# Forgetting attention: the causal mask is added to the diagonal scores by VectorE in PSUM, in place of TensorE's unit matrix times mask

## The chip, the cores and the metric

The kernel runs on one core of a Trainium2 chip. The metric is the time of one execution on the device in microseconds (us), as the median of several runs. Profiles show one execution.

## The reference, cut to what matters

The program is a chain of three layers over 512 positions of width 1024: a Hyena layer, a layer with gated spatial mixing and forgetting attention, and a layer with pooling and a short convolution. All but the first have cross attention to a memory of 256 positions, and each ends in a gated feed-forward block. The change touches the forgetting attention of the second layer, 8 heads of 64:

```python
def forgetting_attention(q, k, v, log_f):
    c = jnp.cumsum(log_f.astype(jnp.float32), axis=1).transpose(0, 2, 1)
    ...
        logits = jnp.einsum('bqhd,bkhd->bhqk', qi, k).astype(jnp.float32) * scale
        logits = logits + ci[..., :, None] - c[:, :, None, :]
        allowed = kpos[None, :] <= qpos[:, None]
        logits = jnp.where(allowed[None, None], logits, -jnp.inf)
        p = jax.nn.softmax(logits, axis=-1)
        return jnp.einsum('bhqk,bkhd->bqhd', p.astype(v.dtype), v)
```

It is swept in 4 query blocks of 128 (qt = 0 to 3). Block qt sees the keys 0 to 128(qt+1) - 1, and only its last 128 keys, the diagonal block, need the mask.

## The kernel before, in words

Weights stream through the whole program: SyncE loads a block of 1 MB into w_raw, ScalarE copies it in two halves to w_hi (L1866), GpSimd computes the rest w_lo (L2331), and TensorE forms each product from three matmuls (hi hi, hi lo, lo hi; L532 to L534). There are two buffers of each. PSUM is two tensors of four banks, `acc` and `aux`, each used round robin. Each engine has its own instruction list, executed in order; semaphores tie them together.

The forgetting attention takes the heads in 4 pairs. The order of the steps is written out by hand in two lists, FOX_PE for TensorE and ScalarE, and FOX_DVE for VectorE. A step is (what, pair p, query block qt). In the text they are S(p,q), T(p,q), O(p) and R(p,q):

- S(p,q), scores. TensorE opens two acc banks, one for each head, and adds up 6 matmuls of half height (64 rows; L906), 2 that subtract the running sum of log f (40 rows; L910), and 2 of full height that add the mask as unit matrix times mask (L913). With n columns, n = 256, 256, 384, 512 for q = 0 to 3. Because the bank must have at least 256 columns, `mask_0` serves q = 0 and `mask_r` the others. VectorE then takes the negative maximum of each row over both banks (L1613), and ScalarE forms the exponentials into prob_e with that as bias and the row sum on the side (L2188); this frees the banks for the S step after the next.
- R(p,q): VectorE takes the reciprocal of the sums (L1617), and GpSimd scales prob_e with it (L2426). In VectorE's list R stands behind the S step that follows its own.
- T(p,q): TensorE transposes the scaled blocks into aux banks (L609), once they are scaled; VectorE copies them to pt (L1620).
- O(p): TensorE multiplies the turned probabilities of pair p with the values (24 matmuls, L885), ScalarE copies the result to ye_hi (L2195), VectorE computes ye_lo (L1173) and frees the aux bank.
- M: the first matmuls of the projection behind the attention, put in ahead of O(2) to fill a wait.

TensorE's order is S(0,0) to S(0,3), then T(0,0) S(1,0) T(0,1) S(1,1) and so on; for p > 0, O(p-1) stands between T(p,1) and S(p+1,1). VectorE's, for one pair in the middle, is T(p,0) S(p+1,0) T(p,1) R(p+1,0) S(p+1,1) O(p-1) T(p,2) R(p+1,1) S(p+1,2) T(p,3) R(p+1,2) S(p+1,3), and R(p,3) is behind S(p+1,0).

The mask tiles are made once, at about 684 us, by four ScalarE copies (L2112, L2114), from a constant that holds 0 where the key is allowed and -1e30 elsewhere. `step` on VectorE lets its instruction raise a semaphore and waits for it before the next instruction; `for_act` raises the one that ScalarE waits for.

Of the kernel before, what the change touches and what calls it, by code (L numbers as in the profile page):

```python
# [28 lines left out]
P = 128  # L29
# [161 lines left out]
def build(nc, ins, out):  # L191
    F32, F32R, I32 = mybir.dt.float32, mybir.dt.float32r, mybir.dt.int32
    ALU = mybir.AluOpType
    ACT = mybir.ActivationFunctionType
# [7 lines left out]
    def at(name, shape, dtype=F32, offset=None):  # L202

        size = 4 * int(np.prod(shape[1:]))
        if offset is None:
            offset = base[0]
            base[0] = -(-(offset + size) // 32) * 32
        assert offset + size <= END, name
        return nc.alloc_sbuf_tensor_at(name, list(shape), dtype, offset=offset)
# [26 lines left out]
    sq_at = base[0]  # L236
# [6 lines left out]
    def c(name, n, lo=0):  # L243
        return ca[:, CA[name] + lo:CA[name] + lo + n]
# [4 lines left out]
    ident = c("ident", P)  # L249

    def area(start=None):

        pos = [region if start is None else start]

        def put(name, shape, dtype=F32):
            t = at(name, shape, dtype, offset=pos[0])
            pos[0] += -(-4 * int(np.prod(shape[1:])) // 32) * 32
            return t
        return put, pos


    put, _ = area()
# [4 lines left out]
    put, pos = area()  # L267
# [45 lines left out]
    put, _ = area()  # L313
# [3 lines left out]
    put, pos = area()  # L317
# [9 lines left out]
    late, _ = area(v_at)  # L327
    q_raw = late("q_raw", [P, TT, T])
    sel_r = put("sel_r", [104, HEADS], F32R)
    ident_r = put("ident_r", [P, P], F32R)  # L330
    sel_raw = put("sel_raw", [104, HEADS])
    row_small = put("row_small", [P, P])
    masks = at("masks", [P, 3 * P], F32R, offset=sq_at)
    mask_r, mask_0 = masks[:, 0:2 * P], masks[:, P:3 * P]
    assert pos[0] <= region + MIXED_AT
    put, pos = area(region + MIXED_AT)
    late, _ = area(pos[0] + 8192)
# [25 lines left out]
    put, pos = area()  # L363
# [21 lines left out]
    put, _ = area()  # L385
# [5 lines left out]
    put, _ = area(region + MIXED_AT)  # L391
# [5 lines left out]
    acc = ctx.enter_context(nc.psum_tensor("acc", [P, 4, 512], F32))  # L397
# [3 lines left out]
    def sem(name):  # L401
        return ctx.enter_context(nc.semaphore(name))
# [6 lines left out]
    acc_ready = sem("acc_ready")  # L409
# [73 lines left out]
    def _(pe):  # L483
# [413 lines left out]
        for what, p, qt in FOX_PE:  # L897
            n = P * (qt + 1)
            if what == "S":
                banks = [open_acc(("S", p, qt, j)) for j in range(2)]  # L900
                scores[0] += 2
                n = max(n, 2 * P)
                for l, r in ((q_hi, k_hi), (q_hi, k_lo), (q_lo, k_hi)):
                    for j in range(2):
                        rows = slice(HD * j, HD * (j + 1))
                        nc.tensor.matmul(banks[j][:, 0:n], l[rows, p, qt * P:(qt + 1) * P], r[rows, p, 0:n],  # L906
                                         start=l is q_hi and r is k_hi, stop=False)
                for j in range(2):
                    h, rows = 2 * p + j, slice(HD * j, HD * j + 40)
                    nc.tensor.matmul(banks[j][:, 0:n], sel_r[rows, h:h + 1].to_broadcast([40, P]), decay_r[rows, 0:n],  # L910
                                     start=False, stop=False)
                for j in range(2):
                    nc.tensor.matmul(banks[j][:, n - 2 * P:n], ident_r[:, :], mask_r if qt else mask_0,  # L913
                                     start=False, stop=True)                        .then_inc(acc_ready, 1)
            elif what == "T":
                pe.wait_ge(probs_scaled, scaled.next(2))
                tiles = [[prob_e[j][qt][:, kt * P:(kt + 1) * P] for kt in range(qt + 1)] for j in range(2)]
                if qt < 2:
                    transposes(("T", p, qt, 0), tiles[0] + tiles[1])
                else:  # L920
                    for j in range(2):
                        transposes(("T", p, qt, j), tiles[j])
            elif what == "O":
                mixed_values(p)
            else:
                mixed_w = block_in(KT, 256)
                mixed_banks = [open_acc(("mixed", o)) for o in range(2)]
                mixed_out(0, range(4))
# [151 lines left out]
    def _(dve):  # L1080
        V = nc.vector
# [14 lines left out]
        def signal_with(ins, counter):  # L1096
            ins.then_inc(counter.sem, 1)
            counter.next()
            newest[0] = counter
# [6 lines left out]
        def for_act(ins):  # L1106
            signal_with(ins, to_act)
# [186 lines left out]
        for b in range(12):  # L1294
            j, part = b // 3, b % 3
# [210 lines left out]
        for t in range(2):  # L1506
            g_rows = g_tok[:, t, :].rearrange("p (g c) -> p g c", g=4)
            scale = row_small[:, 16 + 4 * t:20 + 4 * t].rearrange("p (g one) -> p g one", one=1).to_broadcast([P, 4, P])
# [94 lines left out]
            return aux[:, (n_aux[0] - 1) % 4, :]  # L1603

        exp_done = {}
        for what, p, qt in FOX_DVE + [("O", PAIRS - 1, 0)]:
            n = P * (qt + 1)
            if what == "S":
                dve.wait_ge(acc_ready, acc_done.next(2))
                b = n_acc[0] % 4  # L1610
                n_acc[0] += 2
                exp_done[p, qt] = acc_read.next(2)
                for_act(V.tensor_reduce(small[:, 8 + 2 * qt:10 + 2 * qt], acc[:, b:b + 2, 0:n], axis=AX.X, op=ALU.max,  # L1613
                                        negate=True))
            elif what == "R":
                dve.wait_ge(acc_free, exp_done[p, qt])
                signal_with(V.reciprocal(small[:, 24 + 2 * qt:26 + 2 * qt], small[:, 16 + 2 * qt:18 + 2 * qt]), inverted)  # L1617
            elif what == "T":
                for j in range(1 if qt < 2 else 2):
                    free_aux(V.tensor_copy(turned(p, qt, j), from_bank(next_aux(), qt)))  # L1620
            else:
                bank = next_aux()
                acted()
                halve(ye_hi[:, 4 + p, :], ye_lo[:, 4 + p, :], bank, last=free_aux)
# [220 lines left out]
    def _(act):  # L1845
        S = nc.scalar
# [25 lines left out]
        def step(ins):  # L1872
            ins.then_inc(act_step, 1)
            act.wait_ge(act_step, steps.next())
# [38 lines left out]
        for k in range(KT):  # L1913
            if k == 2:
                split_next()
            n = mark[("x", k)]
# [36 lines left out]
        for b in range(12):  # L1953
            j, part = b // 3, b % 3
# [94 lines left out]
        for k in range(KT):  # L2049
            n = mark[("x again", k)]  # L2050
# [56 lines left out]
        for i in range(4):  # L2107
# [1 line left out]
                split_next()  # L2109
            evacuated()  # L2110
            S.activation(u_t[:, i, :], tmp[i][:, :], ACT.Gelu_apprx_tanh)
        S.activation(ident_r[:, :], ident, ACT.Copy)  # L2112
        for i, scale in ((0, 0.0), (1, 1.0), (2, 0.0)):
            S.activation(masks[:, i * P:(i + 1) * P], c("mask", P) if scale else ident, ACT.Copy, scale=scale)  # L2114
        act.wait_ge(in_even, 16 * 4)
        S.activation(sel_r[:, :], sel_raw[:, :], ACT.Copy)
        split_next()
        for t in range(TT):
            if t == TT - 1:
                split_next()  # L2120
            n = acc_mark[("g", t)]
# [56 lines left out]
        for what, p, qt in FOX_PE + [("O", PAIRS - 1, 0)]:  # L2178
            n = P * (qt + 1)
            if (what, p) == ("O", PAIRS - 1):  # L2180
                split_next()
            if what == "S":
                given()
                for j in range(2):
                    evac.next()
                    i = 2 * qt + j
# [115 lines left out]
        for j in range(2):  # L2302
# [3 lines left out]
            if j == 0:  # L2306
                for g in range(4):
                    n = mark[("pool", g)]
# [242 lines left out]
```

## Time and profile before

| | |
|---|---|
| median of 3 runs | 1920.89 us (1919.56 to 1921.23) |
| span of the profiled execution, first to last instruction | 1918.7 us |
| median less that span | 2.2 us |
| TensorE, VectorE, ScalarE, GpSimd busy | 1889.0, 956.3, 688.7, 913.3 us |
| granted TensorE clock, mean | 0.999 of full speed |
| the mask matmuls, L913 | 32, between 781.9 and 816.1 us |

The time of the profiled execution outside its span is not in the profile; 2.2 us is the median's distance to it. A matmul's row lasts from its start until its result has arrived; the next one starts earlier, so the time it takes from TensorE's queue is read from start to start. "x2" means that a row merges two instructions.

### The profile page before, as it was taken

Reading aid. Unit: us, or ns where it says so; the run is one execution under the profiler, and the core shown is the slowest. Engines: PE = TensorE matmul, PEld = TensorE weight load, DVE = VectorE, ACT = ScalarE, POOL = GpSimd, SP = SyncE. Lnnn points to the kernel's source line nnn. Section 1 sums busy time; section 2 is a strip of 40 time slices with the busy share of each in tenths; the row PEclk is TensorE's granted clock in tenths of the full one; section 3 lists DMA queues with packets and bytes.
Section 4 is the critical chain, followed back from the end, with each engine's and each line's share of the span. In section 5 each row is a group of like instructions: output and inputs, shape, how many; then the busy total and the mean of one; then the engine's idle time right before and its main releaser. Section 6 shows DMA issues by size and latency. Waiting matters only on the chain.

```text
span 1918.7 us, 22821 instructions
## 1 busy us (share of the span) xinstructions
PE 1889.0 (98%) x8677; PEld 1547.8 (81%) x8677; DVE 956.3 (50%) x1245; ACT 688.7 (36%) x1016; POOL 913.3 (48%) x409
## 2 busy tenths in 40 slices
PE   7999999999999999999999999999999999999999
PEld 6777888888888878778778888888888878888887
DVE  7877945444421248654564444213855484444201
ACT  4556333232323344443633232222234543222211
POOL 2564645444444444644544444445445444445442
PEclk9999999999999999999999999999999999999999
DMA  5241122323323322123232232333243223232322
GB/s 178 67 126 66 67 66 88 109 87 93 101 81 102 117 67 98 36 70 128 67 110 87 94 103 85 102 99 100 82 132 110 87 70 107 88 109 87 99 88 77
DMA packets 165176, 178.91 MB, mean 93 GB/s; under 512 B 4697, under 2 KB 152657, under 8 KB 164850
## 3 DMA queue, kind: packets, MB, share of 16 engines
q1 hardware_dynamic: 162092, 172.10, 27.9%
q10 hardware_dynamic: 3013, 5.84, 1.0%
q8 instruction: 48, 0.79, 0.2%
q14 instruction: 23, 0.18, 0.0%
HBM read 175.83 MB, written 2.10 MB: 93 GB/s over the span
## 4 chain that ended last, share of the span: by engine, by line
PE 60%; issue 21%; POOL 12%; DVE 4%; ACT 2%; DMA 0%; POOLq 0%; DVEq 0%; ACTq 0%
PE acc L532 18%; PE acc L534 18%; PE acc L533 18%; POOL w_lo L2331 11%; PE aux L609 1%; PE aux L740 1%; PE acc L740 1%; POOL prob_e L2426 1%; DVE prod L1371 0%; DVE a_lo L1178 0%; PE aux L666 0%; PE acc L906 0%; POOL xp L2415 0%; ACT w_hi L1866 0%; PE aux L532 0%
## 5 line engine op out<-in xcount | busy, mean ns | idle before, releaser
L2331 POOL TENSOR_TENSOR w_lo<-w_raw,w_hi 128x1024 fp32r<-128x1024 f32 x322 | 794.8, 2489 | 865.5 <-ACT w_hi L1866 865.5
L532 PE MATMUL acc<-a_hi,w_hi 128*128 128x512 f32 (+1 forms) x1480 | 580.9, 392 | 2.3 <-DVE a_lo L1178 1.4
L534 PE MATMUL acc<-a_hi,w_lo 128*128 128x512 f32 (+1 forms) x1480 | 577.3, 390 | 0.0
L533 PE MATMUL acc<-a_lo,w_hi 128*128 128x512 f32 (+1 forms) x1480 | 577.1, 390 | 0.0
L1866 ACT ACTIVATE w_hi<-w_raw 128x1024 fp32r<-128x1024 f32 x324 | 324.9, 1051 | 443.5 <-PE acc L534 416.0
L532 PEld LDWEIGHTS acc<-a_hi,w_hi 128*128 128x128 f32 (+1 forms) x1480 | 277.8, 188 | 71.5 <-issue 8.2
L534 PEld LDWEIGHTS acc<-a_hi,w_lo 128*128 128x128 f32 (+1 forms) x1480 | 277.7, 188 | 59.3
L533 PEld LDWEIGHTS acc<-a_lo,w_hi 128*128 128x128 f32 (+1 forms) x1480 | 277.8, 188 | 57.9 <-issue 0.2
L532 PE MATMUL acc<-h_hi,w_hi 128*128 128x512 f32 x528 | 205.8, 390 | 0.0
L534 PE MATMUL acc<-h_hi,w_lo 128*128 128x512 f32 x528 | 205.4, 389 | 0.0
L533 PE MATMUL acc<-h_lo,w_hi 128*128 128x512 f32 x528 | 205.4, 389 | 0.0
L1173 DVE TENSOR_TENSOR h_lo<-tmp,h_hi 128x512 f32 (+1 forms) x66 | 187.9, 2886 | 0.0
L1442 DVE TENSOR_TENSOR tmp<-acc,rstd 128x512 f32<-128x512 f32 x66 | 45.6, 692 | 271.2 <-PE acc L534 271.0
L534 PEld LDWEIGHTS acc<-h_hi,w_lo 128*128 128x128 f32 x528 | 99.1, 188 | 20.7
L533 PEld LDWEIGHTS acc<-h_lo,w_hi 128*128 128x128 f32 x528 | 99.1, 188 | 20.4
L532 PEld LDWEIGHTS acc<-h_hi,w_hi 128*128 128x128 f32 x528 | 99.1, 188 | 20.4
L2072 ACT ACTIVATE tmp<-tmp 128x512 f32<-128x512 f32 x66 | 41.1, 623 | 194.0 <-DVE tmp L1439 194.0
L1439 DVE TENSOR_TENSOR tmp<-acc,rstd 128x512 f32<-128x512 f32 x66 | 45.6, 692 | 92.1 <-PE acc L534 87.5
L2078 ACT ACTIVATE h_hi<-tmp 128x512 f32 (+1 forms) x66 | 41.0, 622 | 135.9 <-DVE tmp L1443 135.9
L1199 DVE TENSOR_TENSOR x<-x,acc 128x512 f32<-128x512 f32 x40 | 27.5, 687 | 119.6 <-PE acc L534 118.8
L1888 ACT ACTIVATE a_hi<-x,param 128x512 fp32r<-128x512 f32 x48 | 34.7, 724 | 119.8 <-DVE x L1199 92.8
L1178 DVE SCALAR_TENSOR_TENSOR a_lo<-x,param,a_hi 128x512 fp32r<-128x512 f32 x48 | 45.6, 951 | 15.7 <-ACT a_hi L1888 10.8
(412 smaller groups left out, 2265.8 us busy)
## 6 DMA issues: line engine op xcount, KB each, us to landing
w_raw<-in_w_gate SPq DMA_DIRECT2D x22, 1024.0 KB, 5.2
w_raw<-in_w_up SPq DMA_DIRECT2D x22, 1024.0 KB, 5.1
w_raw<-in_w_down SPq DMA_DIRECT2D x16, 896.0 KB, 4.8
w_raw<-in_hy_w_in SPq DMA_DIRECT2D x12, 1024.0 KB, 5.7
w_raw<-in_ffn_w_gate SPq DMA_DIRECT2D x11, 1024.0 KB, 5.2
w_raw<-in_ffn_w_up SPq DMA_DIRECT2D x11, 1024.0 KB, 5.2
w_raw<-in_e_w_in SPq DMA_DIRECT2D x10, 1024.0 KB, 5.0
w_raw<-in_xa_wkv SPq DMA_DIRECT2D x8, 1024.0 KB, 5.0
```

Source lines behind the costliest of these rows:

```text
L532: nc.tensor.matmul(o, l_hi, r_hi, start=start, stop=False)
L533: nc.tensor.matmul(o, l_hi, r_lo, start=False, stop=False)
L534: return nc.tensor.matmul(o, l_lo, r_hi, start=False, stop=stop)
L740: last = nc.tensor.matmul(banks[ct][:, ns], y_raw[half][:, 4 * odd + t, ct * P:(ct + 1) * P], inv[:, t, ns], start=t == 0 and not odd, sto ...
L1173: last(V.tensor_tensor(lo, src, hi.bitcast(F32), ALU.subtract))
L1178: for_pe(V.scalar_tensor_tensor(a_lo[:, k, :], x[:, k, :], gain, a_hi[:, k, :].bitcast(F32), ALU.mult, ALU.subtract))
L1439: free_acc(V.tensor_tensor(tmp[j][:, :], take_acc(), rstd[:, :], ALU.mult))
L1442: free_acc(V.tensor_tensor(tmp[2 + j][:, :], take_acc(), rstd[:, :], ALU.mult), again=True)
L1866: S.activation(dst[:, half], w_raw[b % 2][:, half], ACT.Copy).then_inc(w_hi_ready, 1)
L2072: result(S.activation(tmp[j][:, :], tmp[j][:, :], ACT.Silu))
L2078: result(S.activation(h_hi[:, first + j, :], tmp[2 + j][:, :], ACT.Copy))
L2331: nc.gpsimd.tensor_tensor(w_lo[s][:, half], w_raw[s][:, half], w_hi[s][:, half].bitcast(F32), ALU.subtract)\
```

## The change

The two full-height mask matmuls of each S step go, and the decay matmuls close the sum in PSUM. VectorE adds the mask, with PSUM as input and output, to the diagonal 128 columns of both banks in one instruction, and waits for it before the maximum. The unit matrix and the masks in TensorE's format, and the ScalarE copies that made them, go as well.

```diff
@@ buffers
-    ident_r = put("ident_r", [P, P], F32R)
-    masks = at("masks", [P, 3 * P], F32R, offset=sq_at)
-    mask_r, mask_0 = masks[:, 0:2 * P], masks[:, P:3 * P]
@@ TensorE, S step
                     nc.tensor.matmul(banks[j][:, 0:n], sel_r[rows, h:h + 1].to_broadcast([40, P]), decay_r[rows, 0:n],
-                                     start=False, stop=False)
-                for j in range(2):
-                    nc.tensor.matmul(banks[j][:, n - 2 * P:n], ident_r[:, :], mask_r if qt else mask_0,
-                                     start=False, stop=True)                        .then_inc(acc_ready, 1)
+                                     start=False, stop=True).then_inc(acc_ready, 1)
@@ VectorE
+        own_mask = c("mask", P).rearrange("p (one k) -> p one k", one=1).to_broadcast([P, 2, P])
@@ VectorE, S step
                 exp_done[p, qt] = acc_read.next(2)
+                diagonal = acc[:, b:b + 2, n - P:n]
+                step(V.tensor_tensor(diagonal, diagonal, own_mask, ALU.add))
                 for_act(V.tensor_reduce(small[:, 8 + 2 * qt:10 + 2 * qt], acc[:, b:b + 2, 0:n], axis=AX.X, op=ALU.max,
                                         negate=True))
@@ ScalarE
-        S.activation(ident_r[:, :], ident, ACT.Copy)
-        for i, scale in ((0, 0.0), (1, 1.0), (2, 0.0)):
-            S.activation(masks[:, i * P:(i + 1) * P], c("mask", P) if scale else ident, ACT.Copy, scale=scale)
```

## Rows read from the trace of the kernel before

**Rows 1.** The page's busy line: us (share of the span) and instructions of each engine.

```profile
PE 1889.0 (98%) x8677; PEld 1547.8 (81%) x8677; DVE 956.3 (50%) x1245; ACT 688.7 (36%) x1016; POOL 913.3 (48%) x409
```

**Rows 2.** Stretches: length, busy PE, PEld, DVE, ACT, POOL, granted clock, DMA share, GB/s.

```profile
790.00:800.00 10.00, 8.83 (x74) 6.61 (x76) 6.97 (x16) 4.71 (x20) 9.79 (x10) 1.00 0.00 0
800.00:810.00 10.00, 10.00 (x90) 7.45 (x88) 7.45 (x17) 5.31 (x20) 8.71 (x9) 1.00 0.01 2
810.00:820.00 10.00, 10.00 (x76) 7.65 (x74) 7.16 (x15) 4.55 (x15) 8.93 (x9) 1.00 0.12 18
```

**Rows 3.** Timeline, first pair: start, length, engine, instruction, [idle before, releaser].

```profile
783.88 0.69 DVE L1613 TENSOR_REDUCE small<-acc 128x2 f32<-128x512 f32 x1 [1.03 <-PE acc L913]
...
787.45 1.23 DVE L1613 TENSOR_REDUCE small<-acc 128x2 f32<-128x1024 f32 x1 [1.13 <-PE acc L913]
...
788.84 10.95 POOL L2426 TENSOR_SCALAR prob_e<-prob_e,small 128x384 f32<-128x384 f32 x10 [0.60 <-DVE small L1617]
...
794.44 1.09 PE L609 MATMUL aux<-const_a_sb,prob_e 128*128 128x128 f32 x8 [0.87 <-POOL prob_e L2426]
```

**Rows 4.** Timeline, one loop in the middle, from exp(2,2) to exp(3,2).

```profile
805.52 0.58 ACT L2188 ACTIVATE prob_e<-acc,small 128x384 f32<-128x384 f32 x1 [1.43 <-DVE small L1613]
...
806.89 0.19 PEld L906 LDWEIGHTS acc<-k_hi,q_hi 64*128 64x128 f32 x2 [0.17 <-ACT prob_e L2188]
...
809.84 4.26 POOL L2426 TENSOR_SCALAR prob_e<-prob_e,small 128x512 f32<-128x512 f32 x4 [0.34 <-DVE small L1617]
...
811.96 0.69 DVE L1613 TENSOR_REDUCE small<-acc 128x2 f32<-128x512 f32 x1 [1.51 <-PE acc L913]
...
814.35 1.82 POOL L2426 TENSOR_SCALAR prob_e<-prob_e,small 128x256 f32<-128x256 f32 x2 [0.24 <-DVE small L1617]
...
815.14 0.58 ACT L2188 ACTIVATE prob_e<-acc,small 128x384 f32<-128x384 f32 x1 [1.43 <-DVE small L1613]
```

**Rows 5.** Timeline of TensorE: the end of S(2,3), and of S(3,1).

```profile
805.67 0.40 PE L906 MATMUL acc<-k_hi,q_lo 64*128 64x512 f32 x2
805.90 0.40 PE L910 MATMUL acc<-decay_r,sel_r 40*128 40x512 f32 x2
806.24 0.51 PE L913 MATMUL acc<-masks,ident_r 128*128 128x256 f32 x2
806.58 0.38 PE L609 MATMUL aux<-const_a_sb,prob_e 128*128 128x128 f32 x2
...
811.21 0.28 PE L910 MATMUL acc<-decay_r,sel_r 40*128 40x256 f32 x2
811.42 0.50 PE L913 MATMUL acc<-masks,ident_r 128*128 128x256 f32 x2
```

**Rows 6.** Timeline of ScalarE where the mask tiles are made.

```profile
684.53 0.70 ACT L2114 ACTIVATE masks<-const_a_sb 128x128 fp32r<-128x128 f32 x3
...
692.42 2.01 ACT L1866 ACTIVATE w_hi<-w_raw 128x1024 fp32r<-128x1024 f32 x2 [7.10 <-PE acc L534]
```

**Rows 7.** VectorE forms near the addition: min/median/max ns by line; two timeline rows.

```profile
L1281 DVE TENSOR_TENSOR aux<-aux,window x8: 689/690/690, 72.1 to 162.5; 128x512 f32<-128x512 f32 x8
...
184.98 1.23 DVE L1350 TENSOR_TENSOR aux<-aux,odd_part 128x1024 f32<-128x1024 f32 x1 [0.31 <-ACT odd_part L2004]
186.25 1.23 DVE L1351 TENSOR_TENSOR aux<-aux,odd_part 128x1024 f32<-128x1024 f32 x1
...
L1636 DVE SCALAR_TENSOR_TENSOR m_lo<-aux,param,m_hi x16: 473/480/485, 846.8 to 1437.8; 128x256 fp32r<-128x256 f32 x16
```

**Rows 8.** VectorE beside GpSimd: a stretch of the timeline, then min/median/max ns by line.

```profile
317.63 8.02 POOL L2331 TENSOR_TENSOR w_lo<-w_raw,w_hi 128x1024 fp32r<-128x1024 f32 x3
...
320.52 5.68 DVE L1173 TENSOR_TENSOR h_lo<-tmp,h_hi 128x512 fp32r<-128x512 f32 x2
...
L1442 DVE TENSOR_TENSOR tmp<-acc,rstd x66: 691/692/693, 314.0 to 1791.0; 128x512 f32<-128x512 f32 x66
...
L1173 DVE TENSOR_TENSOR ye_lo<-aux,ye_hi x4: 680/686/692, 802.9 to 832.1; 128x512 fp32r<-128x512 f32 x4
```

## The prediction

> **What bounds the kernel now.** I first read the page's busy line: TensorE is busy for 98% of the span, VectorE for 50%, GpSimd for 48% [rows 1]. That is an average over stages, and the change touches only the forgetting attention, from about 781 to 824 us. So the second view is the table by stretch for that stage [rows 2]. There the picture is another one: from 790 to 800 TensorE is busy for only 8.83 of 10 us and GpSimd for 9.79; from 800 to 820 TensorE shows 10.00 of 10, but VectorE is at 7.2 to 7.5 and GpSimd at about 8.8. No engine has much to give, and with 10 us of VectorE counted as 7.45, one pair of heads (9.62 us, below) holds 7.2 us of VectorE.
>
> I write S(p,q), T(p,q) for the steps of pair p and query block q, as in the kernel's two lists, and exp, R, scale for ScalarE's exponentials, VectorE's reciprocal and GpSimd's scaling of that block. The timelines show three regimes.
>
> Until T(0,3), the chain alternates: S(0,1), its maximum on VectorE at 783.88, exp, S(0,3), its maximum at 787.45, which again waited for the mask matmul, R(0,2) queued behind that maximum, then GpSimd without a pause from 788.84 for 10.95 us, and T(0,3), which waited 0.87 us for GpSimd [rows 3].
>
> From T(0,3) to S(2,1) TensorE runs through. From then on TensorE only looks like the bound. Follow one loop [rows 4]: exp(2,2) starts at 805.52; S(3,0) loads its weights at 806.89 and had waited for exactly those exponentials (0.17 us, which is only the hand-over); TensorE runs T(2,1), O(1) and S(3,1); VectorE's maximum of S(3,1) starts at 811.96, released by the mask matmul; ye_lo, the copies of T(2,2), a reciprocal and the maximum of S(3,2) follow with no gap, and exp(3,2) starts at 815.14. That is 9.62 us per pair, and no link in it has slack. TensorE's own queue and this loop through ScalarE and VectorE are equally long, so shortening the one is worth nothing unless the other shrinks too.
>
> **What is removed, and what it gives.** 32 mask matmuls, two in each of 16 S steps. On TensorE's queue the pair takes from its start to that of the transposes behind it: 806.24 to 806.58, 0.34 us [rows 5]; all 16 would be 16 x 0.34 = 5.4 us. For VectorE the scores are complete earlier: the decay matmuls end at 805.90 + 0.40 = 806.30 where the mask ended at 806.24 + 0.51 = 806.75 [rows 5], and at 811.21 + 0.28 = 811.49 against 811.42 + 0.50 = 811.92: 0.45 and 0.43, so 0.44 us.
>
> Is 0.34 real? Between two half-height pairs the step is 0.23 us (805.67 to 805.90), between the decay pair and the full-height mask 0.34 [rows 5]. This 0.11 is a change of tile height. The transposes behind are full height too, so I take it to move to them and save 0.34; if it vanished, the saving would be 0.45; if only the columns' time went (about 2 x 0.11), 0.22. The Trainium skill (TensorEngine Tiling (Array Packing), Key Properties) says that a change of tiling mode drains TensorE; by that rule the 0.11 stays wherever the change falls, which gives 0.34, and without it 0.45. Two such slots lie on the path below, so this is worth 0.2 us either way.
>
> ScalarE loses four copies at 684 us, three of which take 0.70 us together, so some 0.9 in all. It then idles for 7.10 us until TensorE releases it at 692.42 [rows 6], and sel_r is not wanted before 781. Nothing; without that idle time it would be 1 us.
>
> **What is added, and what it costs.** 16 additions over 128x256 elements, PSUM to PSUM with one operand from SBUF. The trace has no such size, but the same form at 512 elements, 0.690 us, and at 1024, 1.23 us [rows 7]: 0.54 us per 512, so 0.42 us at 256. A dependent instruction starts 1.27 us after the 1.23 us one, so 0.04 more: 0.46 us for each addition, in front of the maximum that waits for it and of all that is queued behind (the reciprocal of the step before, the copies out of aux, ye_lo). Bounds: 0.41 if the hand-over is free, 0.52 from the three-operand form at 128x256 (0.48) [rows 7]; and 0 on the path if VectorE's idle 2.4 us per pair swallowed it. I take 0.46, since the loops have no idle VectorE time in them.
>
> Will GpSimd slow it? Two VectorE instructions with both inputs in SBUF took 5.68 us, 2.84 each, while GpSimd ran w_lo [rows 8]. With one input from PSUM, 66 instructions of such a stage all took 691 to 693 ns, and ye_lo in this very stage 680 to 692 [rows 8]. The addition has one input in PSUM: no slowing. The Trainium skill says the same (GPSIMD Engine Reference, Specifications: contention with VectorE instructions in a 2-port mode or with two SBUF inputs); its rule puts this operation outside.
>
> **The sum along the path**, in shifts against the trace (minus is earlier):
> 1. To T(0,3): S(0,1) and S(0,3) are on the chain, each ready 0.44 earlier and 0.46 of addition: 2 x 0.02 = +0.04.
> 2. T(0,3) to exp(2,2): slots of S(1,3) and S(2,0) -0.68, S(2,1) ready -0.44, additions of (2,1) and (2,2) +0.92: -0.20, so -0.16. TensorE itself runs 0.7 to 1 us ahead here for a while.
> 3. R(2,2) stands in front of S(2,3) in VectorE's queue, so the maximum of (2,3) begins with exp(2,2)'s -0.16 and +0.46: +0.30. GpSimd's scaling of (2,3), at 809.84 before [rows 4], starts at 810.14 and then runs (2,3), (3,0), (3,1) without a pause: 4.26 + 1.82 is 6.08 (they start 809.84 and, after 0.24 idle, 814.35 before). End 816.22 against 814.35 + 1.82 = 816.17; the transposes T(3,1), which TensorE reached at about 816.4, can start at 816.3: -0.1.
> 4. The loop of pair 3: slot -0.34, ready -0.44, two additions +0.92, together +0.14; on -0.16 that is -0.02 for exp(3,2), and with the next addition +0.44 for scale(3,3). Its transposes had no slack to spare, but the last of them waited for a PSUM bank anyway; they come out within 0.1 us of where they were. After that TensorE has its projection matmuls back to back and keeps the shift.
>
> Total -0.1 us. The profiled execution has a span of 1918.7, 2.2 below the median of the runs shown (1920.89); the rest lies around the span and isn't touched. So 1920.89 - 0.1 = 1920.8. Five additions and five TensorE terms lie on this path, so it moves by 5 x the error of the addition: -0.35 at 0.41, +0.2 at 0.52.
>
> **The rivals.**
> - All of TensorE's time comes back. 98% busy speaks for it [rows 1], and 10.00 of 10 in two stretches [rows 2]. Then 5.4 us: 1915.5. Against: the loop of [rows 4], and the first third of the stage, where TensorE waits for others. 3 in 100.
> - The additions hide in VectorE's idle 2.4 us per pair: only the path's TensorE terms count, -0.1 - 5 x 0.46 = -2.4, 1918.5. For: VectorE waits for the masks at 783.88, 787.45 and 811.96. Against: each of those waits is already used up by the 0.44. 8 in 100.
> - VectorE becomes the bound (the other side). Per pair 7.2 + 4a us for an addition of a; above 9.62, from a = 0.61, it lengthens every pair. It loses more than 0.2% only from 4 x (7.2 + 4a - 9.62) = 3.84, a = 0.85. The place is the addition beside GpSimd's scaling, which fills 8.7 to 9.8 of 10 us [rows 2]. The two-SBUF form was held for 2.84 - 0.69 = 2.15 us, 0.8 of one GpSimd instruction of 8.02 / 3 = 2.67 [rows 8]; here one takes 10.95 / 10 = 1.1 us [rows 3], so a would be 0.46 + 0.9 = 1.36 and the loss 4 x (7.2 + 5.44 - 9.62) = 12 us: 1933. Against: [rows 8]. 5 in 100; that a lies between 0.6 and 0.85, with 0 to 3.8 us lost, 5 in 100.
> - The removal frees only 0.22 per slot: +0.2, 1921.1, inside my own case.
>
> **How the numbers follow.** The forecast, a time between 1 us less and 1 us more, has the rest, 79 in 100. What a measurement of this kernel can tell from no change is about 0.2%, 3.8 us. Below -3.8 lies only the first rival and what I have missed: 0.04. Above +3.8 the held addition and what I have missed: 0.06. Same 0.90. The range: the runs before scatter from 1919.56 to 1921.23, so about 0.8 each way; the hidden case at 1918.5 and a busier VectorE at +1 to +2 bring it to 1918.7 to 1922.6.
>
> **What would show it.** The additions at 0.42 us each and 6.7 us in all; no mask matmul; the maximum starting 0.46 after the addition. T(0,3) within 0.1 us of 794.44. S(2,1) about 0.7 us early, exp(2,2) only about 0.2 early. VectorE from 7.5 to about 9.2 of 10 us between 800 and 820, and TensorE down from 10.00, now waiting for exp and for GpSimd. ACT's copies at 684 gone with nothing moved. The forecast is wrong if additions come out over 0.6 us, if S(3,0) no longer waits for exp(2,2), or if a stage far from this one moves.

## The result and the profile after

| | before | after |
|---|---|---|
| median of the runs | 1920.32 us (1919.56 to 1921.68, 21 runs) | 1923.42 us (1920.51 to 1924.62, 21 runs) |
| ratio | | 1.0015, interval 1.0009 to 1.0021 |
| span of the profiled execution | 1918.7 us | 1921.6 us |
| its start to S(0,0) | 781.2 | 780.6 |
| the stage: S(0,0) to the first residual addition | 53.2 | 54.7 |
| from there to the end | 1084.3 | 1086.2 |

The kernel got slower by 3.1 us, 0.16%. The forecast was 1920.8 in a range to 1922.6: the effect stayed within the 0.2% that it called no change and gave 90 in 100, but the time lies 0.8 us outside the range. The spans split the loss: 1.5 us inside the stage that was changed, and 2.0 us behind it, where the change touches nothing.

The page's busy line of the kernel after, for [rows 1]:

```profile
PE 1890.1 (98%) x8645; PEld 1547.9 (81%) x8645; DVE 963.1 (50%) x1261; ACT 687.6 (36%) x1012; POOL 913.4 (48%) x409
```

TensorE lost 32 matmuls (8677 to 8645) and is busy for 1.1 us more. Work was taken off an engine and its busy time rose: either what is left waits inside its busy time, or it runs at a lower clock. The stretches of the stage after show the clock (columns as in [rows 2]: length, busy PE, PEld, DVE, ACT, POOL, granted clock, DMA share, GB/s):

```profile
780.00:785.00 5.00, 3.10 (x28) 2.03 (x26) 2.97 (x7) 1.74 (x8) 0.79 (x2) 1.00 0.24 84
785.00:790.00 5.00, 4.66 (x22) 3.05 (x22) 4.02 (x9) 2.48 (x8) 3.24 (x4) 0.56 0.02 3
790.00:795.00 5.00, 4.57 (x24) 3.61 (x25) 3.31 (x9) 2.00 (x10) 5.00 (x5) 0.50 0.00 0
795.00:800.00 5.00, 5.00 (x42) 3.67 (x42) 4.79 (x10) 1.95 (x7) 4.71 (x6) 0.92 0.00 0
...
800.00:810.00 10.00, 8.74 (x82) 6.16 (x80) 8.93 (x20) 5.00 (x19) 8.57 (x9) 1.00 0.01 2
810.00:820.00 10.00, 9.07 (x69) 6.69 (x66) 8.46 (x18) 5.01 (x19) 8.66 (x9) 1.00 0.01 2
```

and those of the kernel before:

```profile
780.00:785.00 5.00, 4.72 (x36) 3.37 (x34) 1.84 (x4) 1.20 (x6) 0.25 (x1) 1.00 0.35 125
785.00:790.00 5.00, 3.73 (x28) 2.56 (x27) 2.98 (x6) 3.15 (x12) 3.91 (x5) 1.00 0.01 3
790.00:795.00 5.00, 3.83 (x31) 3.01 (x32) 3.61 (x8) 2.28 (x11) 5.00 (x6) 1.00 0.00 0
```

Read the granted clock first. Before it is 1.00 throughout. After it is 0.56, 0.50 and 0.92 in three stretches of 5 us, which is (0.44 + 0.50 + 0.08) / 0.5 x 5 = 10.2 us at the lower of the two levels, 1.2 GHz. From 785 to 795 TensorE is busy for 9.23 us with 46 matmuls, where the kernel before was busy for 7.56 us with 59: busier, and doing less. From 800 on, with the clock back at 1.00, the picture is the one forecast: TensorE at 8.74 and 9.07 where [rows 2] shows 10.00, VectorE up from 7.45 and 7.16 to 8.93 and 8.46.

The timeline of TensorE after, on both sides of the fall (start, length, engine, instruction, idle before and releaser):

```profile
782.10 0.39 PE L903 MATMUL acc<-k_hi,q_hi 64*128 64x256 f32 x2 [0.70 <-DVE values L1591]
...
783.73 0.44 PE L903 MATMUL acc<-k_hi,q_hi 64*128 64x384 f32 x2 [0.90 <-ACT prob_e L2182]
...
785.23 0.56 PE L903 MATMUL acc<-k_hi,q_hi 64*128 64x512 f32 x2 [0.53 <-ACT prob_e L2182]
...
794.63 1.64 PE L606 MATMUL aux<-const_a_sb,prob_e 128*128 128x128 f32 x8
...
797.00 0.41 PE L907 MATMUL acc<-decay_r,sel_r 40*128 40x512 f32 x2
```

Ahead of the fall TensorE is in the part where it waits for others: behind S(0,0) there are 0.5 to 0.9 us of idle time before each score step, and between them only matmuls of 64 and 40 rows. The mask matmuls that stood there have 128 rows.

Behind the stage, the stretches of the kernel after that hold both of its later falls:

```profile
900.00:912.00 12.00, 12.00 (x68) 10.62 (x67) 3.76 (x15) 2.17 (x4) 0.54 (x1) 0.86 0.28 87
1488.00:1512.00 24.00, 23.80 (x140) 20.95 (x139) 10.72 (x38) 11.95 (x27) 8.68 (x5) 0.93 0.15 45
```

and the same stretches of the kernel before, in a second profile of it (e10 below):

```profile
900.00:912.00 12.00, 12.00 (x76) 10.82 (x74) 4.81 (x19) 2.10 (x6) 0.00 (x0) 0.86 0.28 87
1488.00:1512.00 24.00, 24.00 (x151) 21.54 (x150) 11.24 (x39) 15.29 (x39) 10.60 (x6) 1.00 0.23 73
```

Near 905 both are at half clock for (1 - 0.86) x 12 / 0.5 = 3.4 us. Near 1496, in the cross attention of the last layer, only the kernel after is: (1 - 0.93) x 24 / 0.5 = 3.4 us. TensorE is busy for 23.8 of the 24 us there, so half the rate for 3.4 us should cost 1.7 us. That is most of the 2.0 us lost behind the stage.

### The profile page after: what moved, and what is told of

Its sections match the earlier page's. It is cut to its first block, busy times and chain, and to the rows that moved or that the text cites. A ratio compares the mean times of both kernels' runs of the same rounds, so it can differ in the third digit from the quotient of the medians.

```text
span 1921.6 us, 22769 instructions
## 1 busy us (share of the span) xinstructions
PE 1890.1 (98%) x8645; PEld 1547.9 (81%) x8645; DVE 963.1 (50%) x1261; ACT 687.6 (36%) x1012; POOL 913.4 (48%) x409
## 4 chain that ended last, share of the span: by engine, by line
PE 60%; issue 21%; POOL 11%; DVE 5%; ACT 2%; POOLq 0%; DMA 0%; DVEq 0%; ACTq 0%
PE acc L529 18%; PE acc L531 18%; PE acc L530 18%; POOL w_lo L2325 11%; PE aux L606 1%; PE aux L737 1%; PE acc L737 1%; PE acc L903 0%; DVE prod L1365 0%; DVE a_lo L1172 0%; PE aux L663 0%; POOL xp L2409 0%; ACT w_hi L1863 0%; PE aux L529 0%; PE aux L531 0%
## 5 line engine op out<-in xcount | busy, mean ns | idle before, releaser
L1172 DVE SCALAR_TENSOR_TENSOR a_lo<-x,param,a_hi 128x512 fp32r<-128x512 f32 x48 | 45.6, 950 | 15.3 <-ACT a_hi L1885 10.2
```

What stands on the lines that cost most here:

```text
L1172: for_pe(V.scalar_tensor_tensor(a_lo[:, k, :], x[:, k, :], gain, a_hi[:, k, :].bitcast(F32), ALU.mult, ALU.subtract))
```

## The experiments

First all of them together. "Stage" and "behind" are the two lower parts of the table above, from each profile; the shift is that of the median against the kernel before on the same chip in the same session.

| kernel | shift of the median, us | ratio, interval | stage | behind | half clock in the stage / behind it, us |
|---|---|---|---|---|---|
| before | | | 53.2 | 1084.3 | 0 / 3.4 |
| after | +3.1 | 1.0015 [1.0009, 1.0021] | 54.7 | 1086.2 | 10.2 / 6.8 |
| e1 no mask at all | -2.1 | 0.9991 [0.9981, 1.0000] | 51.5 | 1082.7 | 6.8 / 0 |
| e2 both | +3.6 | 1.0018 [1.0009, 1.0027] | 56.0 | 1086.1 | 0 / 6.8 |
| e3 10 matmuls more | +1.0 | 1.0004 [0.9995, 1.0013] | 54.4 | 1086.3 | 6.8 / 6.8 |
| e4 pair 0 on TensorE | +0.4 | 1.0003 [0.9994, 1.0012] | 53.4 | 1084.3 | 0 / 3.4 |
| e5 four steps | -0.95 | 0.9998 [0.9989, 1.0007] | 52.3 | 1084.1 | 0 / 3.4 |
| e6 pair 0 without a mask | -0.05 | 1.0000 [0.9990, 1.0009] | 53.1 | 1084.4 | 3.4 / 3.4 |
| e7 pairs 1 to 3 without | +0.4 | 1.0001 [0.9992, 1.0010] | 51.9 | 1082.8 | 0 / 0 |
| e8 24 matmuls more | +1.6 | 1.0009 [1.0000, 1.0018] | 53.4 | 1084.7 | 0 / 3.4 |
| e9 after, again | +3.4 | 1.0017 [1.0008, 1.0026] | 54.6 | 1086.3 | 6.8 / 6.8 |
| e10 before, again | +0.4 | 1.0002 [0.9993, 1.0011] | 53.2 | 1084.3 | 0 / 3.4 |
| e11 four steps, again | -1.4 | 0.9995 [0.9986, 1.0004] | 52.3 | 1085.8 | 0 / 6.8 |
| e12 as e8, half height | +2.0 | 1.0012 [1.0002, 1.0023] | 54.4 | 1086.2 | 3.4 / 6.8 |
| e13 1.6 us later | +3.2 | 1.0015 [1.0006, 1.0024] | 54.9 | 1085.7 | 0 / 6.8 |
| e14 3.2 us later | +3.35 | 1.0018 [1.0009, 1.0027] | 56.5 | 1082.7 | 0 / 0 |

Medians move with the clock stretches of all executions, a profile shows those of one; so mechanisms are read from the stage, and the medians only say what the whole is worth.

How typical a profiled execution is can be told in part. Every execution has its mean granted clock on record, to three decimals, and 3.4 us at half clock lower that mean by 0.5 x 3.4 / 1920 = 0.0009. All 32 executions of the kernel after (with e9) lie at 0.997 or below. Of 131 executions of the kernel before that have it on record, 127 lie at 0.998 or 0.999 and four at 0.997. For these two kernels the profiles are typical. For others they are not: e3's is one of two executions at 0.995, with eight of the other nine at 0.998 or 0.999; e7's is one of three at 1.000, with the other seven at 0.996 or 0.997; e12's has 0.997, with eight of the other nine at 0.998. The mean doesn't tell where in the program the clock was down.

**e1: is it the removal or the addition?** The kernel after without its additions on VectorE.

```diff
-                diagonal = acc[:, b:b + 2, n - P:n]
-                step(V.tensor_tensor(diagonal, diagonal, own_mask, ALU.add))
```

> The mask is left out altogether: no mask matmul and no addition (so each query also sees later keys of its own block). Everything else is as in the changed kernel. Theory A (TensorE's clock: the mask matmuls kept it at full speed in the first third of the attention, and without them it runs some 10 us at half speed): the granted clock falls to 0.5 near 786 us here too, although VectorE has nothing added, and the stage gains far less than the 2.4 us that the sum gave for additions at no cost: median between 1919.5 and 1921.5. Theory B (VectorE's additions are what costs, the clock is a by-product of the waits they make): the clock stays at 1.00 in the stage and the median is 1917.5 to 1918.5.

The stretches of e1:

```profile
780.00:785.00 5.00, 3.31 (x30) 2.29 (x30) 2.46 (x5) 1.83 (x8) 1.14 (x2) 1.00 0.27 94
785.00:790.00 5.00, 4.93 (x26) 3.30 (x28) 3.01 (x8) 3.27 (x12) 3.78 (x5) 0.53 0.01 3
790.00:795.00 5.00, 4.44 (x32) 3.41 (x32) 3.75 (x9) 1.93 (x9) 5.00 (x6) 0.79 0.00 0
```

The clock falls (0.53, 0.79) with nothing added to VectorE, as theory A said. The removal alone does it. The median, 1918.42, is below the range that A gave and inside B's: even with 6.8 us at half clock the stage takes 51.5 us, 1.7 less than before. Where nothing is given to VectorE, the TensorE work is worth something.

**e2: the addition alone.** The kernel before, whose masks stay on TensorE, and VectorE adds the mask once more (cut to the two lines that do it).

```diff
+                diagonal = acc[:, b:b + 2, n - P:n]
+                step(V.tensor_tensor(diagonal, diagonal, own_mask, ALU.add))
```

> The kernel before with VectorE's 16 additions put in as well: the mask is added twice, which leaves the result as it is. TensorE's work is that of before. Theory A: the clock stays at 1.00 through the stage, and only the additions are paid: those of the chain, at least five and at most sixteen of 0.46 us less what hides, so 2.3 to 6 us above before, 1922.6 to 1926.3. Theory B: the same rise, with no way to tell from the clock; if the clock falls here too, longer waits alone are enough for it and A in its plain form is wrong.

```profile
785.00:790.00 5.00, 3.88 (x30) 2.80 (x30) 3.58 (x8) 2.26 (x8) 3.01 (x4) 1.00 0.01 3
790.00:795.00 5.00, 3.95 (x34) 3.04 (x32) 4.15 (x12) 2.71 (x11) 4.42 (x4) 1.00 0.00 0
```

With the masks on TensorE the clock stays at 1.00, and the stage costs 2.8 us more than before (56.0 against 53.2): the price of 16 additions that nothing pays for. The additions don't hide: two of them already make T(0,3) come 0.95 us late, counted from S(0,0).

**e3, e8 and e12: give TensorE its activity back without the masks.** All are the kernel after with matmuls whose result nobody reads, into free slots of aux, placed where TensorE waits. e3 has two ahead of each score step of pair 0 and of S(1,1), 10 in all:

```diff
+            if what == "S" and (p == 0 or (p, qt) == (1, 1)):
+                for _ in range(2):
+                    nc.tensor.matmul(aux[:, n_aux[0] % 4, 0:2 * P], ones_r[:, :], k_hi[:, 0, 0:2 * P],
+                                     start=True, stop=True)
```

> The changed kernel with two matmuls of 128x256 at full height, whose result nobody reads, ahead of the wait of S(0,0) to S(0,3) and S(1,1), written to the aux bank that the next transposes overwrite. They fill TensorE's idle time of 0.5 to 0.9 us there. Theory A: the clock stays at 1.00 in the stage, the maxima and the transposes come as the sum of the prediction had them, and the median falls from 1923.4 to within 1 us of before, 1919.5 to 1921. Theory B: idle time filled changes nothing, 1923 or a little more.

e8 has them ahead of every score step of pairs 0 and 1, and four ahead of each of T(0,2) and T(0,3), 24 in all (against e3):

```diff
-            if what == "S" and (p == 0 or (p, qt) == (1, 1)):
+            if what == "S" and p < 2:
...
+                if p == 0 and qt > 1:
+                    pe.wait_ge(aux_free, n_aux[0] - 3)
+                    for _ in range(4):
+                        nc.tensor.matmul(aux[:, n_aux[0] % 4, 0:2 * P], ones_r[:, :], k_hi[:, 0, 0:2 * P],
+                                         start=True, stop=True)
```

> The changed kernel with two unread matmuls of 128x256 at full height ahead of every S step of pairs 0 and 1, and four ahead of the waits of T(0,2) and T(0,3): 24 in all where the mask had 32, but placed in TensorE's idle time. The first try had ten, and the clock fell at 790 instead of 786. Theory A: now the clock stays at 1.00 through the stage and its length is 52.9 to 53.6 as in before, median 1920 to 1921. Theory B: 54.4 or more, as with ten.

e12 is e8 with the same number of matmuls, the same columns and the same places, over the lower 64 rows of both operands (cut to the operands, against e8):

```diff
-ones_r[:, :], k_hi[:, 0, 0:2 * P]
+ones_r[0:HD, :], k_hi[0:HD, 0, 0:2 * P]
```

> The changed kernel with the same 24 unread matmuls of 256 columns at the same places, but at half height (64 rows of the array instead of 128). With full height the clock held and the stage was 53.4. If the clock goes by how long TensorE works, it holds here as well and the stage is 53.4. If it goes by how much of the array works, it falls again between 785 and 797, and the stage is 54.2 to 54.7.

The stretches of e3:

```profile
785.00:790.00 5.00, 3.52 (x26) 2.42 (x26) 4.32 (x10) 3.12 (x11) 3.89 (x6) 1.00 0.00 0
790.00:795.00 5.00, 4.93 (x26) 3.97 (x27) 3.59 (x10) 1.64 (x8) 5.00 (x5) 0.50 0.01 3
```

of e8:

```profile
785.00:790.00 5.00, 4.29 (x34) 2.95 (x30) 4.13 (x9) 3.11 (x11) 3.87 (x5) 1.00 0.00 0
790.00:795.00 5.00, 4.14 (x35) 3.46 (x36) 4.35 (x11) 2.15 (x10) 5.00 (x5) 1.00 0.02 3
```

and of e12:

```profile
785.00:790.00 5.00, 4.67 (x27) 3.16 (x25) 3.85 (x8) 2.31 (x9) 3.07 (x5) 0.66 0.00 0
790.00:795.00 5.00, 4.08 (x35) 3.40 (x34) 4.40 (x11) 2.46 (x11) 5.00 (x5) 1.00 0.01 3
```

In e3's profile the fall only moves from 785 to 790, and the stage is 54.4; its median, 1921.52, lies between the ranges of its two theories, and most of its executions have a higher mean clock than the profiled one. e8 holds the clock at 1.00, and the stage is 53.4: 1.2 us less than after, although TensorE has 24 matmuls more to do (its median, +1.6 against before, is 1 us above what theory A gave). In e12 the clock falls again (0.66, 3.4 us) and the stage is back at 54.4.

So it is the clock that costs the kernel after 1.2 to 1.3 us of stage (against e8, and against e4 below). What in the 24 matmuls held it is less sure. The profiles of e8 and e12 point to the height: the same matmuls held it on 128 rows and not on 64. But it is one profile each, eight of e12's ten executions have the mean clock of 0.998 that ten of e8's eleven have, and the intervals of the two medians (+1.6 and +2.0) overlap. Also, 0.24 of the 1.0 us between their stages stands there before the fall: the full-height matmuls bring S(0,1) 0.24 us earlier (in e3 too), the half-height ones don't. That height decides is likely, not shown.

**e4, e6 and e7: which masks count?** e4 keeps the masks of pair 0 on TensorE and adds those of pairs 1 to 3 on VectorE:

```diff
-                for j in range(2):
-                    nc.tensor.matmul(banks[j][:, n - 2 * P:n], ident_r[:, :], mask_r if qt else mask_0,
...
+                if p == 0:
+                    for j in range(2):
+                        nc.tensor.matmul(banks[j][:, n - 2 * P:n], ident_r[:, :], mask_r if qt else mask_0,
+                                         start=False, stop=True).then_inc(acc_ready, 1)
...
+                if p > 0:
+                    diagonal = acc[:, b:b + 2, n - P:n]
...
+                        step(V.tensor_tensor(diagonal, diagonal, own_mask, ALU.add))
```

> The four S steps of pair 0 keep the mask on TensorE as before; VectorE adds it for pairs 1 to 3 only. Theory A: up to T(0,0) this is the kernel before, so the clock stays up if those first 5 us decide; then 1919.5 to 1921. If the clock falls somewhat later, in pair 1, the rest of the stage pays a part: 1921 to 1923. Theory B: 12 of 16 additions remain, so about three quarters of the loss: 1922 to 1923.

e6 has TensorE's masks for pairs 1 to 3 and none for pair 0; e7 has TensorE's for pair 0 and none for the others. Neither adds anything on VectorE. In e4's edit to TensorE the condition `p == 0` is `p > 0` for e6 and stays `p == 0` for e7:

```diff
+                if p > 0:
+                    for j in range(2):
+                        nc.tensor.matmul(banks[j][:, n - 2 * P:n], ident_r[:, :], mask_r if qt else mask_0,
```

> The kernel before with the eight mask matmuls of pair 0 left out and nothing put in their place (pair 0 is unmasked, pairs 1 to 3 are masked by TensorE; VectorE adds nothing anywhere). This is less work on every engine. Theory A: the clock falls to 0.5 near 786 us for 6 to 10 us, and the stage comes out longer than before's 53.2 although work was only taken away: 53.5 to 54.5. Theory B: the clock stays up, and S(0,1) and S(0,3), each complete 0.44 us earlier, make the stage 0.9 us shorter: 52.3.

> The complement: TensorE masks pair 0, and pairs 1 to 3 have no mask at all and no addition. Against the version that masks pair 0 on TensorE and adds the others on VectorE (stage 53.4) this takes away just 12 additions. Theory A: clock at 1.00 as there, and the stage is shorter by the additions on the path of pairs 1 to 3, three to six of 0.46: 50.6 to 52.0. Theory B has the same sign, but all 12 additions in sum: 5.5 us, 47.9.

The stretches of e4:

```profile
785.00:790.00 5.00, 3.69 (x28) 2.53 (x26) 3.28 (x7) 3.16 (x11) 3.90 (x5) 1.00 0.01 3
790.00:795.00 5.00, 2.81 (x25) 2.15 (x26) 4.42 (x11) 2.14 (x10) 5.00 (x5) 1.00 0.00 0
```

of e7:

```profile
785.00:790.00 5.00, 3.81 (x29) 2.54 (x26) 3.01 (x7) 3.15 (x11) 3.78 (x5) 1.00 0.01 3
790.00:795.00 5.00, 2.68 (x23) 2.02 (x24) 3.61 (x8) 2.68 (x11) 5.00 (x5) 1.00 0.00 0
```

and of e6:

```profile
785.00:790.00 5.00, 4.04 (x26) 2.50 (x26) 2.31 (x6) 3.06 (x12) 3.01 (x4) 0.77 0.00 0
790.00:795.00 5.00, 4.75 (x39) 3.79 (x38) 3.90 (x10) 2.93 (x11) 4.12 (x4) 0.89 0.01 3
```

With the masks of pair 0 (e4, e7) the clock stays up, even where TensorE is busy for only 2.68 and 2.81 of 5 us; without them (e1, e6, after) it falls. The same holds over all 16 profiles. Nine have pair 0's mask matmuls on TensorE (before, e2, e4, e5, e7, e10, e11, e13, e14), and the clock is at 1.00 in the stage in all nine. Seven do not have them, and it falls in six; the seventh is e8 with its 24 matmuls. The eight mask matmuls of the first pair are the ones that mattered.

e4's stage, with the clock up, is 53.4, and e7's is 51.9: the 12 additions of pairs 1 to 3 cost 1.5 us of stage, about three times 0.46, and the rest is hidden. e6 came out at 53.1, between its two theories: above the 52.3 of the one without a fall, below the 53.5 to 54.5 of the other. Eight matmuls were taken away, nothing was put in their place, and it gained 0.1 us where 0.9 was worked out. The clock was down for 3.4 us only, not for 6 to 10. Nor does the length of the fall set its price here: the kernel after with 10.2 us and e9, the same kernel, with 6.8 us took 54.7 and 54.6.

**e5 and e11: a version for both engines.** VectorE adds where the sum along the path gained from it and TensorE has the mask elsewhere. The edit is that of e4 with another condition:

```diff
+                if (p, qt) in ((1, 3), (2, 0), (3, 0), (3, 1)):
+                    diagonal = acc[:, b:b + 2, n - P:n]
...
+                        step(V.tensor_tensor(diagonal, diagonal, own_mask, ALU.add))
```

> VectorE adds the mask only in S(1,3), S(2,0), S(3,0) and S(3,1), where by the prediction's sum TensorE's slot or the end of its matmuls lies on the path and VectorE's addition hides or comes out even; the other twelve steps keep the mask on TensorE. Theory A (the clock decides up to T(0,3), the sum the rest): clock at 1.00 through the stage, stage (first score matmul to first residual addition) 1.0 to 1.3 us shorter than before's 53.2, so 51.9 to 52.2, and a median of 1919.0 to 1919.8. Theory B (each addition costs about a sixteenth of the loss): 0.4 to 0.8 us above before, 1920.9 to 1921.3.

> The version with VectorE's addition in four steps only, once more, to settle whether it beats before: 1919.2 to 1919.9, 0.6 to 1.2 below before; stage 52.3 at full clock.

Its stage is 52.3 in both profiles, 0.9 to 1.0 less than before and at full clock; 51.9 to 52.2 was expected. The medians are 0.95 and 1.4 us lower (the second, 1918.73, is below the 1919.2 to 1919.9 expected), but neither interval excludes no change. The stage is better than both kernels'; that the whole kernel is, isn't resolved.

**e9 and e10: are the falls behind the stage the kernels' own?** Both kernels unaltered, profiled again.

> The changed kernel once more, unaltered. In its first profile the stage had 10 us at half clock and was 1.5 us longer, which leaves 1.6 of the 3.1 us unexplained; outside the stage that execution had two stretches of some 3.4 us at half clock where before's had one. Theory A: the stage repeats (54.7 within 0.3, clock down from about 785 to 795), the time comes out 2.5 to 3.5 us above before again, and what lies behind the stage is 1082.7 us plus 1.7 for each such stretch, however many there are. Theory B: the stage's length is the same, and what lies behind it is 1 to 2 us longer with no stretch at half clock to show for it.

> The kernel before once more, unaltered: ratio 1.000 within its interval, stage 53.2 within 0.1 and at full clock, and behind it 1082.7 us plus 1.7 for each stretch at half clock. If its stage shows half clock in this second profile, the claim that the mask matmuls keep it up there falls.

The kernel after has a fall near 905 and one between 1495 and 1509 in both profiles; the kernel before has the one near 905 in both, and not the other. Inside the stage e9 was down for 6.8 us, from 791, where the first profile of after had 10.2, from 785.6, and the stage took 54.6 against 54.7.

Over all the profiles, "behind" is 1082.7 plus half of the half-clock time behind the stage, within 0.4 us: 0 gives 1082.7 (e1 1082.7, e7 1082.8, e14 1082.7), 3.4 gives 1084.4 (before 1084.3, e4 1084.3, e5 1084.1, e6 1084.4, e8 1084.7, e10 1084.3), 6.8 gives 1086.1 (after 1086.2, e2 1086.1, e3 1086.3, e9 1086.3, e11 1085.8, e12 1086.2, e13 1085.7). The clock accounts for the differences behind the stage.

**e13 and e14: does a mere shift bring the later fall?** The kernel before, with 7 or 14 matmuls more at M, 1.6 and 3.2 us of TensorE's time, which lengthen the stage by as much and shift all behind it. Nothing else is changed.

```diff
+                for _ in range(7):                         # e14: 14
+                    nc.tensor.matmul(mixed_banks[0], ones_r[:, :], ye_hi[:, 0, :], start=True, stop=True)
```

> The kernel before with seven full-height matmuls of 512 columns that nobody reads, at M, where TensorE never waits: 7 x 0.23 = 1.6 us of plain TensorE work, so everything behind comes 1.6 us later, as in the changed kernel (1.5 us), but with nothing added on VectorE and no half clock. If the later start alone brings a further stretch at half clock into the later stages, the median is 1.6 + 1.7 = 3.3 above before, 1923.5, as in the changed kernel. If not, it is 1.6 above, 1921.9, and the changed kernel's further stretch has another cause.

> The same with fourteen, 3.2 us. If the time outside the attention doesn't depend on when it starts, 3.2 above before, 1923.4. If it does, 1.7 or more on top, or (having slid past) less than 3.2.

The late stretches of e13:

```profile
900.00:912.00 12.00, 12.00 (x66) 10.43 (x65) 2.75 (x14) 2.17 (x4) 1.56 (x1) 0.86 0.26 87
1488.00:1512.00 24.00, 24.00 (x139) 21.26 (x139) 11.19 (x39) 11.73 (x26) 9.27 (x5) 0.93 0.14 45
```

and of e14:

```profile
900.00:912.00 12.00, 12.00 (x69) 10.42 (x68) 4.24 (x15) 2.72 (x6) 4.08 (x2) 1.00 0.28 87
1488.00:1512.00 24.00, 24.00 (x149) 21.38 (x147) 11.78 (x39) 13.14 (x29) 10.60 (x6) 1.00 0.14 45
```

e13 is the kernel before, masks and all, only 1.6 us later, and it has the fall near 1496 that the kernel after has: 3.2 us more in the median for 1.6 us of work. e14, 3.2 us later, has no fall behind the stage in its profile and costs 3.35 us in the median, about its own work. So the fall near 1496 doesn't need the masks to be gone. The later falls change with the time at which that code runs, and not with it alone: e5 and e11 are one kernel with stages alike, and have 3.4 and 6.8 us of half clock behind them. What decides it wasn't found.

## Why the prediction was wrong, and where it was right

**Step 1 failed.** It had T(0,3) within 0.1 us. Counted from S(0,0), T(0,3) came 0.8 us late and S(1,3), right behind it, 1.3, since those transposes took 1.64 us at half clock where [rows 3] shows 1.09 at full. (In e9, where the clock fell later, T(0,3) is 0.1 late and S(1,3) 1.0.) The step's own terms were right as far as they can be seen alone: S(0,3), which starts just ahead of the fall, is 0.03 us late in the kernel after, where 0.02 was forecast; and in e8, with the clock held up, T(0,3) is 0.16 early and S(1,3) 0.08 late. What failed is the silent term that matmuls keep their duration when others are taken away. The clock was among neither the rivals nor the things that would show the forecast wrong, though the table by stretch lists it beside each row.

**The end of step 4 failed the same way.** It said that what stands behind the attention "keeps the shift", so the rest of the program was put at nothing. It was 2.0 us longer, 1.7 of it one more fall.

**Step 2 and the first half of step 3 held in kind.** Counted from S(0,0), S(2,1) comes 0.59 us early in e4 and 0.49 in e8 where 0.7 was said, and TensorE is 0.94 and 0.83 ahead at most, in the 0.7 to 1 us that was said. In the kernel after T(1,2) gains 0.93 against S(1,3), so the same terms act there on top of the 1.3. The slot of a mask pair is the 0.34 us that was taken, not 0.45 and not 0.22: from S(1,3) to T(1,0) is 0.35 shorter in the kernel after and 0.34 in e4 and e8. But from one score step to the next only 0.29 of it is left, so exp(2,2) is 0.07 early in e4 where 0.16 was forecast.

**Step 4 was mis-sized.** The loop from exp(2,2) to exp(3,2) takes 9.86 us in e4 and e8 and 9.87 in the kernel after, against 9.62 before: +0.24 where +0.14 was forecast. So scale(3,3) starts 0.63 late in e4 where 0.44 was said. The step let this vanish, since its transposes waited for a PSUM bank anyway. The timeline of the tail after:

```profile
814.62 0.41 DVE L1609 TENSOR_TENSOR acc<-acc,const_a_sb 128x256 f32<-128x256 f32 x1
815.07 0.96 DVE L1610 TENSOR_REDUCE small<-acc 128x2 f32<-128x768 f32 x1
...
820.85 3.10 POOL L2420 TENSOR_SCALAR prob_e<-prob_e,small 128x512 f32<-128x512 f32 x2 [0.80 <-DVE small L1614]
...
824.01 1.09 PE L606 MATMUL aux<-const_a_sb,prob_e 128*128 128x128 f32 x8 [0.36 <-POOL prob_e L2420]
```

and its last line in e4, with the clock up:

```profile
823.54 1.09 PE L609 MATMUL aux<-const_a_sb,prob_e 128*128 128x128 f32 x8 [0.36 <-POOL prob_e L2434]
```

The last transposes wait 0.36 us for GpSimd in both. The wait for the bank, 0.25 us before, hides only a part. So the edit by itself, without the clock, is worth about +0.2 us in the stage (53.4 in e4 and e8 against 53.2), where the forecast had -0.1. Both stand in for a kernel that wasn't measured: e4 has pair 0's masks on TensorE, e8 has 24 matmuls more.

**The prices held.** The additions, by line (least, median and longest ns):

```profile
L1609 DVE TENSOR_TENSOR acc<-acc,const_a_sb x16: 410/424/433, 781.9 to 817.4; 128x256 f32<-128x256 f32 x16
```

0.424 us where 0.42 was worked out from [rows 7], 16 x 0.424 = 6.8 where 6.7 was said, and the maximum starts 815.07 - 814.62 = 0.45 us after the addition where 0.46 was said. None was held up by GpSimd: the longest is 433 ns, so the rival of 1933 is out. So is the one in which the additions hide (e2: +2.8 in the stage). VectorE came to 8.93 and 8.46 of 10 us where 9.2 was said; from 800 to 820 it waits for the decay matmuls and for ScalarE's exponentials, 0.8 us each. ScalarE's copies are gone and moved nothing: S(0,0) came at 780.6 in the kernel after and at 782.3 in e9, at 781.2 before and at 780.5 in e10.

**"All of TensorE's time comes back"** is out as well: even with no addition anywhere e1 gained 1.7 us in the stage, not 5.4, with part of it given back to the clock.

**The loss, put together.** In the profiles, stage +1.5: about +0.2 of the edit's own and 54.7 - 53.4 = 1.3 from the clock. Behind the stage +2.0, of which 0.5 x 3.4 = 1.7 is one more fall near 1496. With -0.6 ahead of the stage (the two profiles of the kernel before differ by 0.7 there) that is +2.9 of span. The medians, +3.1 and +3.4 in two sessions, leave 1.6 to 2.0 us for what lies outside the stage. The prediction did say that it would be wrong "if a stage far from this one moves"; it had no mechanism for it.

What stays open is what places the later falls. Two profiles of each kernel have the same number of falls behind the stage, and e13 brings the same fall with nothing but 1.6 us of work, so a shift of the stage's end is the likely link between the 1.5 us in the stage and the 1.7 behind it. But the place of the end alone doesn't tell the number of falls: it lies at 836.5 us in e6 and at 836.4 in e13, with 3.4 and 6.8 us of half clock behind it. The link is argued, not shown.

## What to carry to other kernels

Before work is taken off TensorE in a stage where it waits for others, ask whether that work is also what keeps the rest at the high clock. Here it was: eight mask matmuls, some 0.34 us a pair, held it, and they were the only ones of full height in the stage's first 5 us, among matmuls of 64 and 40 rows. Look at the granted clock of each stretch, before and after, ahead of any wait. And price a stage by its own span: in this kernel the total moves by 1.7 us for one half-clock stretch elsewhere, more than all that the edit does by itself.

## What the runs showed of the hardware

- **TensorE's clock falls while it works.** In the kernel after it went to 1.2 GHz while it was busy for 3.10 of 5 us ahead of the fall, with no idle time over 0.9 us, and from S(0,0) on with matmuls of 64 and 40 rows alone. The Trainium skill (TensorE: Matmul & The Clock Gate, HAM oscillation) describes such falls for matmuls broken by long waits for DMAs; here no wait ahead of the fall is over 0.9 us. What separates the profiles is whether pair 0's eight mask matmuls are there (nine of nine hold the clock) or not (six of seven fall). Height may be the reason (e8 and e12), which isn't shown.
- **It falls behind the one-column matmuls too.** The timeline of TensorE after, near 905:

```profile
902.29 0.39 PE L531 MATMUL acc<-a_hi,w_lo 128*128 128x512 f32 x1
902.52 1.84 PE L951 MATMUL aux<-ones,sq_xq 128*128 128x1 f32 x16
904.22 1.14 PE L955 MATMUL aux<-ones,sumsq 128*128 128x1 f32 x8
905.22 0.78 PE L529 MATMUL acc<-a_hi,w_hi 128*128 128x512 f32 x1
905.79 0.63 PE L530 MATMUL acc<-a_lo,w_hi 128*128 128x512 f32 x1
906.22 0.63 PE L531 MATMUL acc<-a_hi,w_lo 128*128 128x512 f32 x1
```

  TensorE counts as busy from 902.52 to 905.2, but with 24 matmuls of one column each. Right behind them a 512-column matmul shows 0.63 us in place of 0.39 and follows its neighbour after 0.43 us in place of 0.23. The same 24 matmuls stand at 1491.98 ahead of the fall near 1496. Leaving out those at the very end, behind the last matmul, the 16 profiles have 28 falls outside the stage, and each starts within 3 us of the last one-column matmul of a run of 8 to 24. They don't bring a fall each time: in e1, e7 and e14 the same matmuls are followed by none behind the stage. A share of busy time doesn't tell whether the clock is down; the step from one matmul to the next does.
- **A lower clock costs what the stage leaves it.** Behind the stage, where TensorE hardly pauses, half of each half-clock microsecond is lost (1082.7, 1084.4 and 1086.1 us with 0, 3.4 and 6.8 us of it). In the stage, 10.2 us of it cost some 1.3 us, and 6.8 us in e9 about as much. Likely TensorE had been waiting for part of that time anyway.
